# A two-layer decoder block on one core: the recurrent stage's norm applied to its products, the last expert's high parts first, the router's weights side by side

## The reference

```
hm = rms_norm(x, moe_norm_g)
g_logits = hm @ w_group                       # 4 groups
g_sel = argmax(g_logits + b_group)            # one group per token
e_logits = (hm @ w_expert)[group g_sel]       # 8 experts of it, the best two kept
x = x + sum over experts of gate * ((silu(hm @ w_gate) * (hm @ w_up)) @ w_down)
```

```
h = rmsnorm(x, g_mix)                          # x * rsqrt(mean(x^2) + eps) * g
rnn_x, rnn_y, conv_b, conv_c, conv_x, gate_rnn, gate_conv = split(h @ w_in)
rnn_x = causal_depthwise_conv(rnn_x, conv4_w) + conv4_b
y_rnn = gelu(rnn_y) * rg_lru(rnn_x, ...)       # gates r and i from block diagonal products
y_conv = conv_b * causal_depthwise_conv(conv_c * conv_x, conv3_w)
merged = sigmoid(gate_rnn) * y_rnn + sigmoid(gate_conv) * y_conv
x = x + merged @ w_out
```

## Time and profile before

| | before |
|---|---|
| median of 3 runs | 982.11 us (981.62 to 982.72) |
| the profiled execution | 981.87 us |
| its span | 980.1 us |
| PE busy | 947.4 us, 97% |
| DVE busy | 741.0 us, 76% |
| ACT busy | 622.1 us, 63% |
| mean granted clock of PE | 0.984 |

### The profile page before, as it was taken

One profiled execution on the slowest core, in us unless ns is written; L12 is line 12 of the kernel. 1 busy time (PEld: TensorE's weight loads), 2 busy tenths in 40 slices (PEclk: granted clock), 3 DMA queues, 4 the chain that ended last, 5 costly groups with the idle time before them and its releaser, 6 DMA issues.

```text
span 980.1 us, 13833 instructions
## 1 busy us (share of the span) xinstructions
PE 947.4 (97%) x5035; PEld 818.1 (83%) x5035; DVE 741.0 (76%) x1083; ACT 622.1 (63%) x949; POOL 20.5 (2%) x40
## 2 busy tenths in 40 slices
PE   6999999989899999999999799999999999999996
PEld 5888888878788888888888699999997788888875
DVE  4567686467699999999999778888797555555575
ACT  4786684565387878877877856656565543444455
POOL 7000000000000000000000000000000000000000
PEclk9999999999799999999999999999999999999999
DMA  9655426225279999999999255637366555565531
GB/s 323 204 167 194 160 87 215 86 87 210 92 276 376 349 368 377 361 357 363 359 370 343 66 175 168 226 128 256 118 220 220 182 191 185 180 205 171 189 111 43
DMA packets 102379, 214.64 MB, mean 219 GB/s; under 512 B 5613, under 2 KB 60161, under 8 KB 96705
## 3 DMA queue, kind: packets, MB, share of 16 engines
q1 hardware_dynamic: 100784, 211.83, 61.4%
q0 software_dynamic: 1392, 2.20, 0.8%
q10 hardware_dynamic: 160, 0.07, 0.0%
HBM read 213.03 MB, written 1.05 MB: 218 GB/s over the span
## 4 chain that ended last, share of the span: by engine, by line
PE 89%; DVE 6%; ACT 3%; issue 1%; DMA 0%; SPq 0%; DVEq 0%; ACTq 0%
PE bank L2092 22%; PE bank L2094 22%; PE bank L2093 21%; PE bank L2626 5%; PE bank L2627 5%; PE bank L2628 5%; PE bank L2097 4%; DVE w_lo L435 1%; DVE w_lo L437 1%; DVE xT_lo L1443 1%; PE bank L2413 1%; DMA xs<-in_mem_dram 0%; PE bank L2414 0%; PE bank L2639 0%; PE bank L2640 0%
## 5 line engine op out<-in xcount | busy, mean ns | idle before, releaser
L2092 PE MATMUL bank<-w_hi,xT_hi 128*128 128x512 f32 (+1 forms) x704 | 280.6, 399 | 4.8 <-DVE w_lo L437 3.2
L2094 PE MATMUL bank<-w_hi,xT_lo 128*128 128x512 f32 (+1 forms) x704 | 275.0, 391 | 0.0
L2093 PE MATMUL bank<-w_lo,xT_hi 128*128 128x512 f32 (+1 forms) x704 | 274.6, 390 | 0.0
L2092 PEld LDWEIGHTS bank<-w_hi,xT_hi 128*128 128x128 f32 x704 | 133.0, 189 | 32.7 <-DVE w_lo L437 5.4
L2094 PEld LDWEIGHTS bank<-w_hi,xT_lo 128*128 128x128 f32 x704 | 132.6, 188 | 27.8
L2093 PEld LDWEIGHTS bank<-w_lo,xT_hi 128*128 128x128 f32 x704 | 132.8, 189 | 25.4
L435 DVE TENSOR_TENSOR w_lo<-stage,w_hi 128x1024 fp32r<-128x1024 f32 (+3 forms) x102 | 117.0, 1147 | 40.2 <-ACT w_hi L421 39.3
L421 ACT ACTIVATE w_hi<-stage 128x1024 fp32r<-128x1024 f32 (+3 forms) x103 | 102.9, 999 | 40.9 <-PE bank L2628 18.7
L2626 PE MATMUL bank<-xT_hi,w_hi 128*128 128x256 f32 x448 | 127.0, 283 | 0.0
L2627 PE MATMUL bank<-xT_lo,w_hi 128*128 128x256 f32 x448 | 126.8, 283 | 0.0
L2628 PE MATMUL bank<-xT_hi,w_lo 128*128 128x256 f32 x448 | 126.8, 283 | 0.0
(11 more groups left out here) (401 smaller groups left out, 1368.3 us busy)
## 6 DMA issues: line engine op xcount, KB each, us to landing
stage<-in_w_in_dram SPq DMA_DIRECT2D x36, 1024.0 KB, 5.0
stage<-in_w_gate_up_dram SPq DMA_DIRECT2D x44, 512.0 KB, 4.5
more<-in_expert_w_down_dram SPq DMA_DIRECT2D x17, 1024.0 KB, 6.8
stage<-in_expert_w_gate_dram SPq DMA_DIRECT2D x33, 512.0 KB, 5.8
stage<-in_expert_w_up_dram SPq DMA_DIRECT2D x33, 512.0 KB, 6.7
more<-in_expert_w_gate_dram SPq DMA_DIRECT2D x31, 512.0 KB, 5.6
more<-in_expert_w_up_dram SPq DMA_DIRECT2D x31, 512.0 KB, 6.5
stage<-in_expert_w_down_dram SPq DMA_DIRECT2D x15, 1024.0 KB, 7.0
```

What stands on the lines that cost most here:

```text
L2092: mm(o, k_hi, v_hi, start=start, stop=False)
L2093: mm(o, k_hi, v_lo, start=False, stop=False)
L2094: return mm(o, k_lo, v_hi, start=False, stop=stop)
```

## The change

Five things are changed.

1. The router. `r_hi` and `r_lo` lie side by side in `r_parts`, so a block's high part meets both in one matmul of 72 columns, and its low part meets `r_hi` in one of 36. The two sums lie side by side in PSUM, and DVE adds them in `choose_group` before it applies the norm's factor. moe2 and moe3 are turned after two blocks rather than four, and moe3 has bank 7. DVE takes the second add to x between low parts 0 and 1, and low part 2 ahead of the norm's factor. ACT makes high parts 2 and 3 and the root ahead of `raw_high`.
2. The last expert. ACT makes the last down unit's two chunks ahead of the tanh, and the high parts of the units U_HEADS and U_HEADS + 1 in the places that fall free; DVE takes both low chunks ahead of `aT_lo`. PE begins `down_by_chunks` with high by high when `aT_hi` is there, and waits for `aT_lo` after it.
3. `bring_back` does the high parts of a pair of sums as soon as `y_hi` is there, then the low parts.
4. The recurrent stage. PE turns x itself. The norm's factor is a number for each token, which is a column in these products (tokens lie along the row): so DVE spreads `rstd` over 128 columns (`row_wide`), PE turns it in the midst of the first head's GELU unit (`turn_scales`, product "scales"), DVE copies the row (`scale_row`, the same on each partition) and squares it (`scale_row2`).
5. In each head DVE multiplies by the row: RX into `xpad` (in place of ACT's copy), GELU's product into `y_in`, `cpad` by the squared row, the two gates, and y_conv. ACT's two copies of GELU's product become one square, and its two tanhs of the gates read what DVE wrote. PE's first head is written out ahead of the loop. POOL's load of `p_in`, which waited for the scaled halves of x, waits for the first `rx_hi`.

The diff, cut to what the prediction speaks of:

```diff
--- before.py
+++ after.py
-HEAD_LINKS = 15
+HEAD_LINKS = 16
@@ the router, PE
-            if half:
-                turn("moe", x, [("x_cross", 2)], (2, 3))
 ...
             for k in range(4 * half, 4 * half + 4):
+                if k == 2:
+                    turn("moe", x, [("x_cross", 2)], (2, 3))
                 if k % 2 == 0:
                     been_read(pe, f"moe{k // 2}")
                 kk = at_k("moe", k)
                 for t in range(T):
-                    ins = three(b[:, CHOICES * t:...], xT_hi[...], xT_lo[...], r_hi[:, k], r_lo[:, k], ...)
+                    at = 2 * CHOICES * t
+                    mm(b[:, at:at + 2 * CHOICES], xT_hi[...], r_parts[:, k].rearrange("p w n -> p (w n)"), ...)
+                    ins = mm(b[:, at:at + CHOICES], xT_lo[...], r_hi[:, k], ...)
@@ the router, DVE
-        low_parts("moe", MOE_G, (0, 1))
+        low_parts("moe", MOE_G, (0,))
         add_chunk(1, C_CO, U_CO + 3, "x_cross")
+        low_parts("moe", MOE_G, (1,))
         chunk_squares(1)
+        low_parts("moe", MOE_G, (2,))
 ...
-        low_parts("moe", MOE_G, (2, 3))
+        low_parts("moe", MOE_G, (3,))
@@ choose_group, DVE
+            then(nc.vector.tensor_copy(biased[:], both[:, 1]))
+            ins = tt(logits[:], both[:, 0], biased[:], ALU.add)
+            frees(ins, "router")
+            been_read(dve, "router")
@@ the last expert, ACT (tanh_high)
+                if last_down_unit is not None:
+                    for c in range(2):
+                        chunk_hi(act, last_down_unit, c, st)
                 act.wait_ge(st.unit_done, g * PER_TURN + (up_unit(base, j) + 1))
 ...
+                if last_down_unit is not None and splits[0]:
+                    splits[0]()
                 act.wait_ge(sem(name + "_turned"), eighths(g, j + 1))
                 nc.scalar.activation(flat3(aT_hi[:])[:, 0:FF], bank[7][:, 0:FF], ACT.Copy)...
+                if last_down_unit is not None and splits[1]:
+                    splits[1]()
@@ the last expert, PE
             def down_by_chunks(g, u0):
-                pe.wait_ge(sem(name + "_aT_lo"), eighths(g, LAST + 1))
                 for c in range(2):
+                    pe.wait_ge(sem(name + "_aT_hi"), eighths(g, LAST + 1))
                     for k in range(2):
-                        ins = down_block(LAST, s, k, c)
+                        mm(o, hi[:, P * k:P * k + P], w_hi[:, s, at[k]:at[k] + 512], start=False, stop=False)
+                    pe.wait_ge(sem(name + "_aT_lo"), eighths(g, LAST + 1))
+                    pe.wait_ge(st.lo_ready, u0 + 1)
+                    for k in range(2):
+                        mm(o, lo[...], w_hi[...]); ins = mm(o, hi[...], w_lo[...])
@@ the start of the recurrent stage, ACT
+        mix_squares(0, 0)
+        high_parts("mix", MIX_G)
+        mix_squares(0, 1)
+        mix_squares(1, 0)
+        mix_squares(1, 1).then_inc(sem("norm_sums"), 1)
         roots("mix")
-        for t in range(T):
-            nc.scalar.activation(xs[:, t, 512:1024], x[:, t, 512:1024], ACT.Copy, scale=rstd[:, t:t + 1])...
-        high_parts("mix", MIX_G)
-        split_hi(act, SLOT, U_HEADS + 1)
@@ the same, DVE
+        low_parts("mix", MIX_G)
+        split_lo(dve, SLOT, U_HEADS + 1)
         dve.wait_ge(sem("norm_sums"), nth(NORMS, "mix"))
 ...
-        for t in range(T):
-            ts(xs[:, t, 0:512], x[:, t, 0:512], rstd[:, t:t + 1], None, ALU.mult)...
+        nc.vector.tensor_copy(row_wide, rstd[:].unsqueeze(2).to_broadcast([P, T, P])).then_inc(sem("row_wide"), 1)
 ...
+        b = product(dve, "scales")
+        then(nc.vector.tensor_copy(scale_row, b[:, 0:256]))
+        ins = tt(scale_row2, scale_row, scale_row, ALU.mult)
@@ the same, PE
-        turn("mix", xs, [("mix_scaled", T)], (0, 1))
-        turn("mix", xs, [("mix_right", T)], (2, 3))
+        turn("mix", x, [("x_moe", 2)], (0, 1))
+        turn("mix", x, [("x_moe", 4)], (2, 3))
@@ a head, ACT
             unit(C_CONV)
-            done(RX)
-            nc.scalar.activation(xpad[:, :, 3:259], blocks(bank[0]), ACT.Copy).then_inc(sem("rx_copied"), 1)
             unit(X_CONV)
             act.wait_ge(sem("conv4_done"), h + 1)
             nc.scalar.activation(rx_hi[:], ...)
-            done(GELU)
-            nc.scalar.activation(y_sq[:], bank[1][:, :], ACT.Square)
-            nc.scalar.activation(y_in[:], bank[1][:, :], ACT.Copy).then_inc(sem("y_copied"), 1)
             unit(RG_R)
+            act.wait_ge(sem("y_scaled"), h + 1)
+            nc.scalar.activation(y_sq[:], y_in[:], ACT.Square, scale=...).then_inc(sem("y_squared"), 1)
+            done(C_CONV)
+            nc.scalar.activation(c_in[:], bank[2][:, :], ACT.Copy).then_inc(sem("c_copied"), 1)
             act.wait_ge(sem("gelu_inner"), h + 1)
             nc.scalar.activation(y_tanh[:], y_sq[:], ACT.Tanh, ...)
-            done(C_CONV)
-            nc.scalar.activation(c_in[:], bank[2][:, :], ACT.Copy)...
@@ a head, DVE
+            def scaled(dst, src, row):
+                return tt(by_feature(dst[:]), by_feature(src[:, :]), over_both(row), ALU.mult)
             unit(C_CONV)
+            done(RX)
+            tt(xpad[:, :, 3:259], by_feature(bank[0][:, :]), over_both(scale_row), ALU.mult)...
             dve.wait_ge(sem("rx_copied"), h + 1)
 ...
-            link(ts(y_sq[:], y_sq[:], 0.044715, 1.0, ALU.mult, ALU.add))
-            tt(y_sq[:], y_sq[:], y_in[:], ALU.mult).then_inc(sem("gelu_inner"), 1)
+            done(GELU)
+            scaled(y_in, bank[1], scale_row).then_inc(sem("y_scaled"), 1)
             unit(RG_R)
+            dve.wait_ge(sem("y_squared"), h + 1)
+            stt(y_sq[:], y_sq[:], 1.0, y_in[:], ALU.add, ALU.mult).then_inc(sem("gelu_inner"), 1)
 ...
             dve.wait_ge(sem("cx_read"), h + 1)
+            link(tt(cpad[:, :, 2:258], cpad[:, :, 2:258], over_both(scale_row2), ALU.mult))
 ...
+            done(G_R)
+            scaled(gr_tanh, bank[5], scale_row).then_inc(sem("gates_scaled"), 1)
             done(B_CONV)
-            tt(y_conv, bank[4][:, :], y_conv, ALU.mult).then_inc(sem("b_read"), 1)
+            link(tt(y_conv, bank[4][:, :], y_conv, ALU.mult))
+            tt(conv3[:], conv3[:], over_both(scale_row), ALU.mult)
 ...
+            done(G_C)
+            scaled(gc_tanh, bank[6], scale_row).then_inc(sem("gates_scaled"), 1)
             split_lo(dve, SLOT, U_HEADS + 10, UNITS_HEAD, h)
@@ a head, PE
+                        if first and j == GELU and f == 0 and k == 4:
+                            turn_scales()
```

More of the change, by code:

```diff
@@ L461, in program @@
                 + ["qc0", "qc1", "cs00", "cs01", "qc2", "qc3", "cs10", "cp00", "cp01", "cs11", "co00", "co01", "cp10", "cp11"]
-                + ["catc0", "catc1", "co10", "co11", "catc2", "catc3", ("moe0", 4), ("moe1", 5), ("router", 6), ("moe2", 4), ("moe3", 5), ("rank", 7)]
-                + [f"mix{n}" for n in range(4)]
+                + ["catc0", "catc1", "co10", "co11", "catc2", "catc3", ("moe0", 4), ("moe1", 5), ("router", 6), ("moe2", 4), ("moe3", 7), ("rank", 7)]
+                + [f"mix{n}" for n in range(4)] + [("scales", 4)]
                 + [("ffn0", 6), ("ffn1", 7), ("ffn2", 6), ("ffn3", 7), ("pT", 7), ("ple0", 4), ("ple1", 5), ("ple2", 6), ("ple3", 7)])
@@ L661, in choose_group @@
             for t in range(T):
-                ins = ts(logits[:, t], b[:, CHOICES * t:CHOICES * t + CHOICES], rstd[:, t:t + 1], None, ALU.mult)
-            frees(ins, "router")
+                ins = ts(logits[:, t], logits[:, t], rstd[:, t:t + 1], None, ALU.mult)
+            then(ins)
         def place_tokens():
@@ L1196, in swiglu, with experts @@
             split_hi(act, SLOT, U_GATE)
-        def experts(name, st, base, groups, nth_tail, before_tail=None, before_sums=None):
+        def experts(name, st, base, groups, nth_tail, before_tail=None, splits=(None, None)):
             for k in range(KD):
@@ L2391, in _ @@
                 for t in range(T):
-                    ins = three(b[:, CHOICES * t:CHOICES * t + CHOICES], xT_hi[:, kk, P * t:P * t + P], xT_lo[:, kk, P * t:P * t + P],
-                                r_hi[:, k], r_lo[:, k], start=False, stop=k == KD - 1 and t == T - 1)
+                    at = 2 * CHOICES * t
+                    mm(b[:, at:at + 2 * CHOICES], xT_hi[:, kk, P * t:P * t + P], r_parts[:, k].rearrange("p w n -> p (w n)"),
+                       start=False, stop=False)
+                    ins = mm(b[:, at:at + CHOICES], xT_lo[:, kk, P * t:P * t + P], r_hi[:, k],
+                             start=False, stop=k == KD - 1 and t == T - 1)
         fills(ins, "router")
@@ L2469, in down_by_chunks @@
                 s = u0 % RING
-                pe.wait_ge(sem(name + "_aT_lo"), eighths(g, LAST + 1))
+                hi, lo = (flat3(v[:]) for v in (aT_hi, aT_lo))
                 for c in range(2):
-                    if c:
-                        pe.wait_ge(st.lo_ready, u0 + 1)
+                    o, at = bank[4 + c][:, :], [D * k + 512 * c for k in range(2)]
```

(24 more changed lines are left out.)

118 lines of the change are left out of this document (53 added, 65 removed).

## The result

Over four runs of each kernel in one session the changed one took 987.68 us (987.22 to 988.88) and the one before 982.41 us: ratio 1.0056, interval 1.0039 to 1.0074. The change makes the kernel 5.3 us slower. Forecast were 983.3 us, and 978.5 to 987.5 as the range. The profiled execution has a span of 985.4 us, 5.3 more than 980.1.

A forecast was written before the change was run, and what follows sets the result against it. PE was taken as the bound, 43.18 us a head, with a DVE-ACT chain only 1.20 us shorter. Terms -3.6 - 1.8 + 5.9 + 0.2 + 0.5 = +1.2 us on 982.11 gave 983.3 us, range 978.5 to 987.5.

The forecast's parts named there:

- Router: In the router, 16 of 48 matmuls go and DVE applies its factor at 248.3 for 251.9: -3.6 us.
- Last expert: At the last expert's down product, PE starts on `aT_hi` 0.45 us sooner; part of a joint -1.8 us.
- Start of the heads: Between last expert and heads, PE turns x from 548.9 without waiting for the norm; rest of the joint -1.8 us.
- Heads: DVE's added multiplies stretch a head to 45.9 us: +5.9 over three cycles, +0.2 from there to w_out's second half.
- The chain of handovers: In each head, DVE and ACT wait on each other in a chain of 41.98 us, 1.20 shorter than PE's.
- Clock: At the heads' start, PE's scattered short work may drop it to 1.2 GHz: 0 or 1.2 us, taken as +0.5.
- the clock takes the start back: Rival, chance 0.22: low PE clock through RX and half of GELU, +3.3 in place of +0.5, 986 us.
- The price of a multiplication: In the heads, each added 128x512 DVE multiply costs 0.60 to 0.85 us, with nothing added for reading PSUM.

## Why the prediction was wrong

- **Router** (-3.6): -4.1, the right size with luck in it. I took 0.21 us for a product as a rate set by the instruction. That it doesn't depend on the columns is right (72 and 36 are alike below), but 0.21 us was the price at half clock. In the changed kernel PE made the first products 0.11 us apart at full clock, and only the last five 0.21 us apart; waits of 0.68 and 0.18 us for low parts took back some of the gain. PE's timeline there, then its windows:

```profile
242.67 0.28 PE L2409 MATMUL bank<-r_parts,xT_hi 128*128 128x72 f32 x1
242.78 0.26 PE L2411 MATMUL bank<-r_parts,xT_lo 128*128 128x36 f32 x1
...
246.23 0.38 PE L2411 MATMUL bank<-r_parts,xT_lo 128*128 128x36 f32 x1
246.44 0.41 PE L2409 MATMUL bank<-r_parts,xT_hi 128*128 128x72 f32 x1
```

```profile
242.00:244.00 2.00, 1.50 (x15) 1.40 (x13) 1.70 (x5) 1.87 (x6) 0.00 (x0) 1.00 1.01 363
246.00:247.20 1.20, 1.03 (x5) 0.92 (x5) 0.06 (x1) 1.18 (x2) 0.00 (x0) 0.50 1.05 430
```

- **Last expert** (the 0.5 within -1.8): right in the trace (hidden part turned to first add to x: 542.36 to 547.99 before, 538.54 to 543.70 after, 5.63 and 5.16 us), not to be seen in the time.
- **Start of the heads** (the other -1.3): this step failed. "PE turns the first pairs of x from 548.9", 545.3 with the router's gain, should have read 549.0. I took it that PE, freed from the norm, starts as soon as x is there, and read the 3.95 us of wait for `xs` as the whole price of what stands between the two stages. The last semaphore names only the latest of the things that PE needed; its own jump, by the estimate above 0.5 us earlier, stood behind it. What is late next once the wait is gone was worked out for DVE and ACT, and not for PE's own program, although the block lies right between the two lines that I compared. Without the block the step measures 12.9 us for the forecast 12.7.
- **Heads** (+5.9, +0.2): right to a tenth: 137.62 us for three cycles, and 5.3 - 5.07 = 0.2 from lo(C_CONV) of head 3 (698.84 for 693.77) to the end. PE's waits in a head are 0.19, 0.83 and 0.90 us for the 0.5, 1.1 and 1.1 forecast. The chain of handovers had 1.20 us to spare, not the 5.7 us that DVE idles. With most of the added work gone PE sets the pace at once.
- **Clock** (+0.5): 0.6 in this stretch, but for another reason, so the size is luck. It fell behind 4.5 us of an idle PE, not among short matmuls: without the gap PE runs the same transpositions and products at 1.00. Of the rival "the clock takes the start back" the half clock from 549 to 553 did come and ended before 556; the start's loss was mostly the gap.
- **The price of a multiplication** was right. Two of the added ones in DVE's timeline of the changed kernel, the first from a bank, the second from SBUF:

```profile
563.50 0.68 DVE L1960 TENSOR_TENSOR xpad<-bank,xs 128x512 f32<-128x512 f32 x1
...
577.74 0.69 DVE L1986 TENSOR_TENSOR cpad<-cpad,xs 128x512 f32<-128x512 f32 x1
```

The 0.065 us more for PSUM that the Trainium skill gives (VectorE: DVE Perf Modes, "The TRN2 errata") is not there.

The sum by stretches of the two profiled executions: first add to x 547.99 to 543.70, -4.3; to lo(C_CONV) 14.00 to 17.52, +3.5; three heads +5.8; the rest +0.2; together +5.3 us, the difference of the spans.

## What to carry to other kernels

A wait that the profile shows may stand in front of another that it does not: before a wait is removed, list all that the engine does between its last work and its next, jumps over blocks that are never executed among it, and ask what each takes once nothing hides it. Idle time of an engine is cover only as far as the chain through the other engines leaves it: read the spare time from the one wait that points at the bound engine (1.20 us of 5.7 here). And price the parts of a change one by one, for this one held a gain of 4 us together with a loss of 9.

## What the hardware did that I had not expected

- A jump on PE over 352 products that aren't executed left it 4.5 us without work; the same over 170 cost 0, 3.1 or 4.5 us by its place in the program; two jumps in a row 6.35, three 7.84. In the profile it is a wait "issue" at the next instruction, and a 16 KB packet of the instruction queue moves in it, 1.5 us before PE goes on (546.42 to 547.5, then 549.04).
- PE went back over a loop of 360 products, nearly three such packets, without a gap and without a packet (none from 598 to 747 us in the kernel before).
- A GpSimd multiplication of 128x512 with both inputs in SBUF held up the VectorE instruction beside it by 1.1 us in three of four cases (0.41 to 1.53 and 1.22 to 2.33 for subtractions), without a wait in the profile: the delay is in the busy time.
- PE's clock was 1.00 for 16 transpositions that followed its last products by 0.5 us, and 0.77 to 0.50 when they followed by 4.5 us: 2.29 us for them against 3.20 to 3.65.
- PE's router products of 72 and of 36 columns both took 0.11 us from start to start at a granted clock of 1.00, and 0.21 at 0.50.
